# Finding the chosen experts with a match-and-replace and a comparison, and moving the combination weights behind the first selection

## The reference

```
t = h.reshape(B * S, D)
logits = (t @ w_router + b_router).astype(jnp.float32)      # 256 tokens x 32 experts
top_v, top_i = lax.top_k(logits, TOP_K)                     # TOP_K = 4
top_w = jax.nn.softmax(top_v, axis=-1)
combine = jnp.sum(jax.nn.one_hot(top_i, N_EXPERTS) * top_w[..., None], axis=1)
...
def expert_step(acc, p):                                    # once for each of the 32 experts
    u = t @ w1 + b1                                         # 1024 -> 2048
    g = jnp.minimum(u[:, :D_FF], 7.0)
    lin = jnp.clip(u[:, D_FF:], -7.0, 7.0)
    a = g * jax.nn.sigmoid(1.702 * g) * (lin + 1)
    y = a @ w2 + b2                                         # 1024 -> 1024
    return acc + ce[:, None] * y, None
```

## Time and profile before

| | before |
|---|---|
| median of 3 runs | 1379.04 us (1377.87 to 1379.08) |
| the profiled execution | 1378.92 us, of which the span of its instructions 1377.1 us |
| mean granted TensorE clock | 0.994 |
| PE busy | 1322.0 us (96%), 6521 instructions |
| PEld busy | 682.9 us (50%) |
| DVE busy | 476.3 us (35%), 806 instructions |
| ACT busy | 327.3 us (24%) |
| moved by DMA | 475.06 MB, mean 345 GB/s |

### The profile page before, as it was taken

One profiled execution on the slowest core, in us unless ns is written; L12 is line 12 of the kernel. 1 busy time (PEld: TensorE's weight loads), 2 busy tenths in 40 slices (PEclk: granted clock), 3 DMA queues, 4 the chain that ended last, 5 costly groups with the idle time before them and its releaser, 6 DMA issues.

```text
span 1377.1 us, 16094 instructions
## 1 busy us (share of the span) xinstructions
PE 1322.0 (96%) x6521; PEld 682.9 (50%) x6521; DVE 476.3 (35%) x806; ACT 327.3 (24%) x478; POOL 21.4 (2%) x39
## 2 busy tenths in 40 slices
PE   7999999999999999999999999999999999999995
PEld 7889997988888333333333333333333332333331
DVE  4754545444656322322223222322232222222223
ACT  5465545464344100110011000100010001110002
POOL 2000000000101000000000000000000000000000
PEclk9999999999999999999999999999999999999998
DMA  9354343646559899999999999999999999999993
GB/s 308 129 195 170 135 172 123 217 150 221 189 225 358 357 426 428 425 426 429 427 427 429 427 427 429 427 427 429 427 427 429 427 428 428 427 427 428 427 427 163
DMA packets 68233, 475.06 MB, mean 345 GB/s; under 512 B 8480, under 2 KB 10592, under 8 KB 43616
## 3 DMA queue, kind: packets, MB, share of 16 engines
q1 hardware_dynamic: 66048, 473.01, 83.6%
q10 hardware_dynamic: 2144, 1.47, 0.4%
HBM read 473.42 MB, written 1.05 MB: 345 GB/s over the span
## 4 chain that ended last, share of the span: by engine, by line
PE 78%; DMA 16%; ACT 2%; DVE 2%; SPq 1%; issue 1%; ACTq 0%; DVEq 0%
PE bank L1473 41%; PE bank L1297 17%; DMA place<-in_w_exp_in 15%; PE bank L1286 7%; PE bank L1558 4%; PE bank L1486 1%; ACT fxqT L808 1%; PE bank L1530 1%; PE bank L1502 1%; DMA fxv<-in_mem 1%; PE bank L1522 1%; PE bank L1474 1%; PE bank L1410 1%; PE bank L1429 1%; DVE w_lo L870 0%
## 5 line engine op out<-in xcount | busy, mean ns | idle before, releaser
L1473 PE MATMUL bank<-place,fxqT 128*64 128x512 f32 x1536 | 688.7, 597 | 28.0 <-ACT fxqT L808 15.5
L1474 PE MATMUL bank<-place,fxqT 128*64 128x512 f32 x1536 | 688.7, 597 | 0.0
L1473 PEld LDWEIGHTS bank<-place,fxqT 128*64 128x64 f32 x1536 | 199.0, 137 | 429.5 <-issue 386.3
L1150 DVE TENSOR_SCALAR big_a<-bank 128x512 f32<-128x512 f32 x32 | 22.1, 691 | 532.4 <-PE bank L1474 532.4
L870 DVE TENSOR_TENSOR w_lo<-ring,w_hi 128x2048 fp32r<-128x2048 f32 x64 | 146.6, 2291 | 155.5 <-ACT w_hi L571 155.4
L1474 PEld LDWEIGHTS bank<-place,fxqT 128*64 128x64 f32 x1536 | 199.0, 137 | 0.0
L571 ACT ACTIVATE w_hi<-ring 128x2048 fp32r<-128x2048 f32 x64 | 122.8, 1919 | 160.2 <-PE bank L1297 113.9
L805 ACT ACTIVATE big_a<-big_a 128x512 f32<-128x512 f32 x32 | 20.2, 630 | 442.4 <-DVE big_a L1150 442.4
L1178 DVE TENSOR_TENSOR xs<-bank,xs 128x512 f32<-128x512 f32 x132 | 81.9, 683 | 24.3 <-PE bank L1558 24.3
L1297 PE MATMUL bank<-w_hi,h_hi 128*128 128x512 f32 x224 | 88.3, 394 | 0.1
L1297 PE MATMUL bank<-w_hi,h_lo 128*128 128x512 f32 x224 | 87.3, 390 | 0.0
(11 more groups left out here) (272 smaller groups left out, 1281.5 us busy)
## 6 DMA issues: line engine op xcount, KB each, us to landing
place<-in_w_exp_in SPq DMA_DIRECT2D x128, 2048.0 KB, 31.3
place<-in_w_exp_out SPq DMA_DIRECT2D x64, 2048.0 KB, 31.9
ring<-in_w_in SPq DMA_DIRECT2D x19, 2048.0 KB, 8.0
ring<-in_w_branch SPq DMA_DIRECT2D x6, 2048.0 KB, 7.9
ring<-in_w_mem_kv SPq DMA_DIRECT2D x4, 2048.0 KB, 8.1
ring<-in_w_out SPq DMA_DIRECT2D x2, 2048.0 KB, 12.1
ring<-in_w_in SPq DMA_DIRECT2D x2, 1024.0 KB, 8.3
xs<-in_x SPq DMA_DIRECT2D x2, 512.0 KB, 4.2
```

The lines of the kernel that those rows point to most:

```text
L1150: dve.tensor_scalar(gate.rearrange("c (q p) -> c q p", q=4), bank[0][:, :].rearrange("c (p q) -> c q p", q=4), LIMIT, None, ALU.min).then_ ...
L1473: mm(o[0:CAP, :], lhsT, low, start=start, stop=stop)
L1474: return mm(o[CAP:P, :], lhsT, high, start=start, stop=stop)
```

## The change

The mask is found on the logits themselves. The logits get four more columns that hold -3e38 (`NONE`), and so do columns 8 to 11 of `top`. One `match_replace` for each tile takes the four largest and the four pads as the eight values to be matched, and writes `left`, a copy of the logits in which each of them is replaced by -2e38 (`TAKEN`). `mask` is then one comparison of `left` with `TAKEN` for both tiles. The position search, the conversion and the one-hot rows are gone. Slot numbers now count from 1, so that `rank` needs no subtraction and its fill is 0. The rank products raise `rank_done` before the two products of the totals, which go to bank 5 and raise `totals_done`. The combination weights are made by `combine()` after the first selection and the busiest total; they are exponentials of all 32 logits times the mask, divided by their sum. Four fills (`pads_ready`) are made behind `turn_out(3)`. ACT scales tile 1 of the residual into `tn` ahead of the Exp table's load. Of the `keep_clock` calls, the three ahead of `score` go, ten become six and twelve become three. `gather` waits for each tile's selection apart.

```diff
-            warm(ACT.Exp)
-            act.wait_ge(topm_ready, 1)
+            act.wait_ge(rstd_ready, 1)
+            act.activation(tn[:, 1, :], xs[:, 1, :], ACT.Copy, scale=rstd[:, 1, 0:1]).then_inc(scaled_act, 1)
+            warm(ACT.Exp)
+            act.wait_ge(topm_ready, 1)
             for t in range(TT):
-                act.activation(topw[:, t, :], top[:, t, 0:TOPK], ACT.Exp, bias=negmax[:, t:t + 1],
-                               accum_out=esum[:, t:t + 1]).then_inc(topw_exp, 1)
-            act.activation(tn[:, 1, :], xs[:, 1, :], ACT.Copy, scale=rstd[:, 1, 0:1]).then_inc(scaled_act, 1)
+                act.activation(exps[:, t, :], logits[:, t, 0:NE], ACT.Exp, bias=negmax[:, t:t + 1]).then_inc(exps_ready, 1)
...
             turn_out(3)
+            dve.memset(rank[:, :, NE:NE + 2], 0.0).then_inc(pads_ready, 1)
+            dve.memset(comb[:, :, NE:NE + 2], 0.0).then_inc(pads_ready, 1)
+            dve.memset(logits[:, :, NE:NE + TOPK], NONE).then_inc(pads_ready, 1)
+            dve.memset(top[:, :, 8:8 + TOPK], NONE).then_inc(pads_ready, 1)
+            dve.wait_ge(pads_ready, 4)
             dve.wait_ge(squares, 2 * 2 + 2 * 2)
...
-                step(dve.max(top[:, t, :], logits[:, t, :]))
-                step(dve.max_index(topi[:, t, :], top[:, t, :], logits[:, t, :]))
-            step(dve.tensor_copy(topf[:, :, :], topi[:, :, :]))
+                step(dve.max(top[:, t, 0:8], logits[:, t, 0:NE]))
+                step(dve.match_replace(left[:, t, :], top[:, t, :].rearrange("p (a j) -> p a j", a=2)[:, :, 0:TOPK],
+                                       logits[:, t, :], TAKEN))
+            dve.tensor_scalar(mask[:, :, :], left[:, :, 0:NE], TAKEN, None, ALU.is_equal).then_inc(mask_ready, 1)
             dve.tensor_scalar(negmax[:, :], top[:, :, 0:1].rearrange("p t o -> p (t o)"), -1.0, None,
                               ALU.mult).then_inc(topm_ready, 1)
-            (two one-hot comparisons and their sum into mask, L1094 to L1099)
             dve.tensor_scalar(tn[:, 0, :], xs[:, 0, :], rstd[:, 0, 0:1], None, ALU.mult).then_inc(scaled, 1)
-            (two fills and the combination weights, L1101 to L1110)
             dve.wait_ge(rank_done, 1)
...
-            step(dve.tensor_scalar(rank[:, :, 0:NE], rank[:, :, 0:NE], 1.0, None, ALU.subtract))
+            def combine():
+                dve.wait_ge(exps_ready, 2)
+                step(dve.tensor_tensor(comb[:, :, 0:NE], exps[:, :, :], mask[:, :, :], ALU.mult))
+                step(dve.tensor_reduce(esum[:, :], comb[:, :, 0:NE], AX.X, ALU.add))
+                step(dve.reciprocal(rsum[:, :], esum[:, :]))
+                step(dve.tensor_tensor(comb[:, :, 0:NE], comb[:, :, 0:NE],
+                                       rsum[:, :].unsqueeze(2).to_broadcast([P, TT, NE]), ALU.mult))
...
                 select(r, 0)
                 if isinstance(r, int):
-                    dve.tensor_reduce(most[:, :], bank[4][:, 192:224], AX.X, ALU.max).then_inc(route_ready, 1)
+                    dve.wait_ge(totals_done, 1)
+                    dve.tensor_reduce(most[:, :], bank[5][:, 0:NE], AX.X, ALU.max).then_inc(route_ready, 1)
+                    combine()
...
-            keep_clock(0, 3)
...
-            keep_clock(2, 10)
+            keep_clock(2, 6)
             pe.wait_ge(mask_ready, 1)
...
-            mm(bank[4][:, 160:192], before[:, :], mask[:, 1, :], start=False, stop=True)
-            mm(bank[4][:, 192:224], ones[:, :], mask[:, 0, :], start=True, stop=False)
-            mm(bank[4][:, 192:224], ones[:, :], mask[:, 1, :], start=False, stop=True).then_inc(rank_done, 1)
-            keep_clock(2, 12)
+            mm(bank[4][:, 160:192], before[:, :], mask[:, 1, :], start=False, stop=True).then_inc(rank_done, 1)
+            mm(bank[5][:, 0:NE], ones[:, :], mask[:, 0, :], start=True, stop=False)
+            mm(bank[5][:, 0:NE], ones[:, :], mask[:, 1, :], start=False, stop=True).then_inc(totals_done, 1)
+            keep_clock(2, 3)
...
-                pe.wait_ge(sel_ready, k)
                 for t in range(TT):
+                    pe.wait_ge(sel_ready, k - 1 + t)
```

More of the change, by code:

```diff
@@ L7 @@
 I32 = mybir.dt.int32
-U32 = mybir.dt.uint32
 ALU = mybir.AluOpType
@@ L34 @@
 CAP = 64
+NONE, TAKEN = -3.0e38, -2.0e38
 PUT_BANKS = (7, 3, 0, 1)
@@ L222, in build @@
         selW = sb("selW", [P, TT, 2, CAP])
[L223 to L228, removed]
+        logits = sb("logits", [P, TT, NE + TOPK])
+        left = sb("left", [P, TT, NE + TOPK])
+        top = sb("top", [P, TT, 16])
+        exps = sb("exps", [P, TT, NE])
         mask = sb("mask", [P, TT, NE])
@@ L307, in build @@
         dve_step = sem("dve_step")
-        tT_ready, logits_done, topm_ready, topw_exp = (sem(n) for n in ("tT_ready", "logits_done", "topm_ready", "topw_exp"))
-        mask_ready, rank_done, route_ready = (sem(n) for n in ("mask_ready", "rank_done", "route_ready"))
+        logits_done, pads_ready, topm_ready, exps_ready = (sem(n) for n in ("logits_done", "pads_ready", "topm_ready", "exps_ready"))
+        mask_ready, rank_done, totals_done, route_ready = (sem(n) for n in ("mask_ready", "rank_done", "totals_done", "route_ready"))
         sel_ready, selW_ready, gather_done, got_ready = (sem(n) for n in ("sel_ready", "selW_ready", "gather_done", "got_ready"))
@@ L481, in _ @@
                                    fill=-1e30, base=0, pattern=[[-1, P]], channel_multiplier=1).then_inc(consts, 1)
-            pool.iota(slots_f[:, :], [[1, CAP * (ROUNDS + 1)]], base=0, channel_multiplier=0,
+            pool.iota(slots_f[:, :], [[1, CAP * (ROUNDS + 1)]], base=1, channel_multiplier=0,
                       allow_small_or_imprecise_dtypes=True).then_inc(consts, 1)
@@ L1086, in _ @@
                 dve.wait_ge(logits_done, t + 1)
-                step(dve.scalar_tensor_tensor(out=logits[:, t, :], in0=bank[t][:, 0:NE], scalar=rstd[:, t, 0:1],
+                step(dve.scalar_tensor_tensor(out=logits[:, t, 0:NE], in0=bank[t][:, 0:NE], scalar=rstd[:, t, 0:1],
                                               in1=br[:, :], op0=ALU.mult, op1=ALU.add))
-                step(dve.max(top[:, t, :], logits[:, t, :]))
-                step(dve.max_index(topi[:, t, :], top[:, t, :], logits[:, t, :]))
@@ L1093, in _ @@
                               ALU.mult).then_inc(topm_ready, 1)
[L1094 to L1097, removed]
@@ L1098, in _ @@
-            dve.tensor_reduce(mask[:, :, :], hot[:, :, :, :].rearrange("p t j e -> p t e j"), AX.X,
-                              ALU.add).then_inc(mask_ready, 1)
             dve.tensor_scalar(tn[:, 0, :], xs[:, 0, :], rstd[:, 0, 0:1], None, ALU.mult).then_inc(scaled, 1)
[L1101 to L1104, removed]
             dve.wait_ge(mask_ready, 1)
[L1106 to L1109, removed]
@@ L1110, in _ @@
-            step(dve.tensor_reduce(comb[:, :, 0:NE], hot[:, :, :, :].rearrange("p t j e -> p t e j"), AX.X, ALU.add))
             dve.wait_ge(rank_done, 1)
```

## The result

The changed kernel takes 1367.07 us (median of 4 runs, 1366.06 to 1367.90) against 1379.06 us before (median of 4): a ratio of 0.9913 (95% interval 0.9901 to 0.9926), 12.0 us faster, where 3.8 us and 1375.2 were forecast. It is faster, but by three times what was forecast, and the time lies outside the range of 1374.3 to 1377.0. The profiled execution took 1366.06 us with a span of 1364.3, 12.8 under the span of before.

A forecast was written before the change was run, and what follows sets the result against it. The prediction took the weight stream to set the end, moving one to one with the first expert's start. Terms 0.43 - 0.04 + 1.33 + 2.08 = 3.80 us gave a median of 1375.2 us, range 1374.3 to 1377.0.

The forecast's parts named there:

- what bounds the kernel: Whole kernel: the weight stream sets the end, running dry before the eleventh piece, so 3.80 us won in routing passes on.
- the signs of being wrong: Granted clock under 1.00 between 438 and 460 us, DVE last before the first expert, or end moving less than eleventh issue.
- the filler ahead of the scores: Before the router's scores: dropping three `keep_clock` calls wins 0.43 us, bounds 0 and 0.67.
- the fills: Four fills on DVE ahead of `rstd`: 0.40 us, covered by DVE's idling before the logits, so cost 0.
- logits to mask: Scores to mask on DVE: match-and-replace loses 0.04 us, one comparison replacing conversion and one-hot steps wins 1.33.
- mask to gather: From mask's end to gather: 4.11 us becomes 2.03, PE's filler ending last; 2.08 won, bounds 1.9 and 2.3.
- what is moved behind the gather: DVE's `combine` steps after the selection: covered by 0.26 us at the worst before the first expert, so cost 0.
- the lower bounds: All terms' bounds on the unfavourable side: a gain of 2.7 us, ending at 1376.3.
- the transfers hide it: Rival at the weight stream: if it were not dry, the end would stay at 1379.0 us; chance 0.05.
- DVE is late beside the gather: Rival behind the mask: late DVE eats its 0.26 us cover and more; gain about 3.0, 1376.0 us; chance 0.12.
- restart faster: Rival at the eleventh piece: warm queues save part of the ramp, up to 0.8 us more, 1374.4; chance 0.06.
- The clock: Rival in routing: fewer PE fillers drop the clock, costing 2.8 us, 1378.0, or 1383.2 if it oscillates; chance 0.09.

The follow-up runs named there:

- the nine kernels on the boundary: Kernels with weight buffers starting on a multiple of 256 bytes: the changed kernel, the kernel before moved by 480 bytes, and their variants; medians 1367.07 to 1373.54 us.
- the weights first: Changed kernel with the combination weights made ahead of the rank again, by the new four steps: 1369.05 us.
- the kernel before with the new fillers: Kernel before, weight buffers moved by 480 bytes onto the boundary, with the change's filler calls (0, 6 and 3): 1373.54 us.
- without fillers: Changed kernel without any filler calls in the routing (the six and the three removed): 1369.04 us.
- the run that keeps six calls: Changed kernel without the three filler calls behind the rank products, the six ahead of the mask kept: 1367.92 us.
- the four kernels off the boundary: Kernel before (1378.85 us) and the changed kernel with buffers moved by 32, 128 and 224 bytes (1374.52, 1374.01, 1375.04 us).
- the eight on it that have no filler at the start: Kernels with buffers on a multiple of 256 bytes, except the changed kernel with sixteen more filler calls behind the first projection slot (1368.35 us).

## Why the prediction was wrong

**The step that failed** is in the part on what bounds the kernel: "From there the stream has a fixed number of bytes to move at one rate. The end therefore moves with the first expert's start, one to one." The first half is true of the bytes, not of the rate. The rate hangs on where the buffers begin, and the new tiles moved them onto a multiple of 256 bytes. That is worth 7.0 us of the 12.0, and no term of the sum stood for it. Nor did one stand for the stretch ahead of the routing, which ended 1.2 to 1.9 us sooner. Among the signs of being wrong I listed an end that moves less than the eleventh issue; it moved more, by 12.8 us against 5.75. A hint was there: the diff gives the tiles' sizes, and packets that took 612 to 621 ns for the same 16 KB were in the trace of before, though no row of it says where the spread comes from. I read the stream's rate and never what it was made of.

**What held.** The stream ran dry ahead of the eleventh piece and did not hide the routing; in the nine kernels on the boundary the eleventh piece is issued between 452.62 and 460.18 us, and the end follows 911.16 to 912.04 us later, so one to one within 0.9 us. The terms, forecast and measured: the filler ahead of the scores 0.43 and 0.51; the fills 0 and 0; logits to mask 1.29 and 1.34; mask to gather 2.08 and 2.01 (from the chain); what is moved behind the gather 0 and -0.02. Together 3.80 and 3.84. One sum was slightly off: the lower bounds add up to 2.8 us, not 2.7. The sentence of the Trainium skill on the pipe that must empty ("VectorE: DVE Perf Modes", "The DRAIN you can't avoid") would have cost 0.2 us by the prediction's estimate. These fills start 10 to 20 ns apart, so the rows decide against it here; the same section excepts an operation that nothing holds back, which the prediction left out.

**The rivals.** That the transfers hide it, that DVE is late beside the gather: neither came. The stream did not restart faster either (its first bytes come between 0.9 and 1.1 us behind the issue in both kernels); it ran faster throughout. The clock did not fall in the changed kernel, but the rival's mechanism is real, and at a price under the 2.8 us that it was given at most: the fall cost 1.6 us with the weights first, 1.7 in the kernel before with the new fillers, and 2.4 without fillers (14.62 less the 12.24 of the run that keeps six calls). So the change can't do without all nine calls, and it can without the last three; whether fewer than six would hold the clock was not tried.

**What stays open.** The stretch to the last projection ended 1.92 us sooner in the profiled pair, and by the medians some 1.2 (12.0 less 3.84 and 7.0). Over the profiled executions that stretch ended between 437.69 and 439.42 us in the four kernels off the boundary, and between 436.24 and 438.86 in the eight on it that have no filler at the start. Two things bear on it. The ring buffers moved along, and the traces show that their transfers gained too: the 2 KB packets that fill them took 92.6 to 92.7 ns on average off the boundary and 91.0 to 91.6 on it (31744 packets, 2 to 3 us over 16 engines, of which only what PE waits for counts). And ahead of the routing the clock stood at 1.2 GHz for some 7 us in some executions, both of the profiled pair among them, and for some 10 us in others. Among those with 7 us the kernels on the boundary reach the end of the last projection 1.3 us sooner on average (436.66 against 437.93), among those with 10 us 0.5 us (438.50 against 439.04). With one profiled execution of each kernel this is a sign, not a proof: the ring and the expert buffers were moved together in every run.

## What to carry to other kernels

Before costing a change that adds or drops a tile, work out where the tiles behind it now begin: a stream that sets the end can gain or lose more by that than the edit itself. Look at the durations of equal packets: here a spread in them (612 to 621 ns, where 611 was possible) went with a placement that cost 7 us. A gain that hangs on two chains (here DVE's steps and PE's filler) was won only when both were cut, 3.84 us against 0.86 with DVE's alone, and a filler that holds the clock is part of the cost of cutting the work around it.

## What the hardware showed that was not expected

A 16 KB packet into a partition row took 611 ns (10th to 90th percentile; mean 614) when the row began on a multiple of 256 bytes, and 611 to 621 ns (mean 618) when it began 32, 128 or 224 bytes past one: 0.7% of the stream's rate, 428 against 431 GB/s, 7 us of this kernel. Taking nine short filler calls out of a routing of 12.5 us brought the granted clock from 2.4 to 1.2 GHz and made it 14.6 us long; taking out the last three did not.
